# Two modulation chunks moved into dead tiles piece by piece, output weights awaited by halves, one value projection cut in two, and the first tile's store moved behind the last gather

## What is computed

```python
mod = silu(c) @ w_ada + b_ada
sh1, sc1, g1, sh2, sc2, g2 = split(mod, 6)
h = x * (1 + sc1) + sh1
qa, ka, va, qb, kb, vb = split(h @ w_in)
ya = rms_norm(moba_attention(qa, ka, va, bias))
yb = rms_norm(dilated_attention(qb, kb, vb, bias))
x = layer_norm(ALPHA * x + (1 + g1) * (concat(ya, yb) @ w_out))
h2 = x * (1 + sc2) + sh2
# router: 8 heads, top 16 of 128 x 128 product keys
q = h2 @ w_q
s1, s2 = q @ sub_keys, top 16 of each, top 16 of their 256 sums -> e, g
f = sum over 128 experts (gelu(h2 . u[e]) * g) * v[e]
x = layer_norm(ALPHA * x + (1 + g2) * f)
```

## Time and profile before

| | |
|---|---|
| device time, median of 3 runs | 826.3 us (824.68, 826.3, 827.65) |
| the profiled execution: time / span | 824.76 us / 823.0 us |
| busy share: TensorE, VectorE, ScalarE, GpSimd | 83%, 71%, 41%, 36% |
| gathers (GpSimd's queue) | 268.45 MB |
| all other loads and stores (SP's queue) | 54.55 MB |
| mean DMA rate over the span | 393 GB/s |

### The profile page before, as it was taken

How to read it: one execution, slowest core, us unless ns; L and a number is a source line. 1 busy time by engine, 2 the same in 40 slices (tenths; PEclk the granted TensorE clock), 3 DMA queues, 4 the chain that set the end, 5 groups by cost and what they waited for, 6 DMA issues and landing times.

```text
span 823.0 us, 7304 instructions
## 1 busy us (share of the span) xinstructions
PE 686.9 (83%) x1984; PEld 326.1 (40%) x1984; DVE 583.0 (71%) x1348; ACT 340.5 (41%) x989; POOL 295.0 (36%) x262
## 2 busy tenths in 40 slices
PE   8999979899997979696989777877868787878785
PEld 4887635554444544352323223322322222223221
DVE  4666967877798777777777878757675767675455
ACT  0012323476646343444445345444343434353333
POOL 1000000234346545454455443544344443434330
PEclk9999989999999989899989997999999999999999
DMA  9999995699999999999999999999999999999992
GB/s 304 376 403 413 420 418 207 261 347 374 385 392 411 422 421 422 421 422 421 422 421 422 420 422 412 406 423 421 422 422 420 422 422 421 420 422 422 422 420 93
DMA packets 56925, 323.74 MB, mean 393 GB/s; under 512 B 6130, under 2 KB 16690, under 8 KB 20402
## 3 DMA queue, kind: packets, MB, share of 16 engines
q0 software_dynamic: 37008, 268.45, 79.2%
q1 hardware_dynamic: 18994, 54.55, 17.2%
q10 hardware_dynamic: 882, 0.27, 0.2%
HBM read 322.18 MB, written 1.07 MB: 393 GB/s over the span
## 4 chain that ended last, share of the span: by engine, by line
DMA 48%; PE 34%; DVE 8%; issue 4%; ACT 4%; POOL 1%; DVEq 0%; SPq 0%; ACTq 0%
DMA ring<-in_experts,e_all 45%; PE bank L518 19%; PE bank L507 7%; PE bank L540 4%; DMA ring<-in_w 4%; DVE acc L1008 3%; DVE ring L858 3%; ACT diag L707 1%; PE bank L622 1%; PE bank L603 1%; POOL ring L1160 1%; ACT weight L698 1%; ACT gel L694 1%; PE bank L610 1%; DVE T_h L871 0%
## 5 line engine op out<-in xcount | busy, mean ns | idle before, releaser
L518 PE MATMUL bank<-ring,diag 128*128 128x512 f32 x952 | 475.5, 636 | 107.9 <-ACT diag L707 107.1
L1160 POOL DMA_INDIRECT ring<-in_experts,e_all x255 | 289.1, 1134 | 501.2 <-PE bank L518 297.1
L518 PEld LDWEIGHTS bank<-ring,diag 128*128 128x128 f32 x952 | 174.7, 198 | 387.3 <-ACT diag L707 228.2
L858 DVE CUSTOM_DVE_ANT_0 ring<-ring,T_h 128x1024 f32<-128x1024 f32 x128 | 156.7, 1225 | 111.7 <-DMA ring<-in_experts,e_all 111.7
L858 DVE CUSTOM_DVE_ANT_0 ring<-ring,h 128x1024 f32<-128x1024 f32 x128 | 156.7, 1224 | 70.8 <-DMA ring<-in_experts,e_all 68.6
L694 ACT ACTIVATE gel<-pre 128x1 f32<-128x1 f32 x256 | 51.8, 202 | 327.8 <-DVE pre L858 327.2
L707 ACT ACTIVATE diag<-consts,weight 128x128 f32<-128x128 f32 x238 | 95.5, 401 | 7.8
L698 ACT ACTIVATE weight<-gel,g_all 128x1 f32<-128x1 f32 x256 | 75.4, 295 | 9.3
L1008 DVE SCALAR_TENSOR_TENSOR acc<-ring,cact,acc 128x512 f32<-128x512 f32 x63 | 47.4, 752 | 5.8 <-DMA ring<-in_w 3.0
L507 PE MATMUL bank<-ring,hT_yT 128*128 128x512 f32 x80 | 35.6, 596 | 0.8 <-DMA ring<-in_w 0.7
L540 PE MATMUL bank<-hT_yT,lnw 128*128 128x256 f32 x128 | 28.7, 380 | 0.9 <-DVE hT_yT L975 0.9
(11 more groups left out here) (178 smaller groups left out, 556.3 us busy)
## 6 DMA issues: line engine op xcount, KB each, us to landing
ring<-in_w SPq DMA_DIRECT2D x18, 1024.0 KB, 13.7
ring<-in_w SPq DMA_DIRECT2D x12, 512.0 KB, 10.5
H_s<-in_w SPq DMA_DIRECT2D x6, 1024.0 KB, 14.4
ring<-in_w SPq DMA_DIRECT2D x16, 256.0 KB, 7.0
lnw<-in_w SPq DMA_DIRECT2D x4, 1024.0 KB, 17.3
ring<-in_experts,e_all POOLq DMA_INDIRECT x255
H_s<-in_w SPq DMA_DIRECT2D x5, 512.0 KB, 9.1
lnw<-in_w SPq DMA_DIRECT2D x4, 512.0 KB, 8.5
```

The source lines that it names most:

```text
L518: last = nc.tensor.matmul(tile_sum(t)[n], diag[:, m % DIAGS, :], ring[:, RING_AT[i], D + CH * n:D + CH * n + CH], start=(s == 0), stop=(s ...
L858: nc.vector.tensor_tensor_reduce(ring[:, r, 0:D], ring[:, r, 0:D], h2[i // SLOTS], 1.0, 0.0, ALU.mult, ALU.add, pre[:, i % PAIR:i % PAIR + ...
L1160: nc.gpsimd.indirect_dma_start(ring[:, r, :], None, A["experts"], bass.IndirectOffsetOnAxis(ap=e_all[:, i:i + 1], axis=0)).then_inc(slot_i ...
```

## The change

1. Chunk 10 is no longer loaded into the ring. It comes in three pieces: 2 rows into `QT_h2T[:, 0:D]`, 2 into `hT_yT[:, 0:D]`, 4 into `H_s[:, 0:2D]`. Chunk 11's pieces are 2 rows in xT_y, 1 in V_x1, 1 in diag, 4 in `H_s[:, 2D:4D]`.
2. Their sums are cut: `wsuma 11` (4 rows), `wsuma 10 0` and `wsuma 10 1` (2 each), later `wsumb 10` and `wsumb 11` (4 each). `patch_read` counts them, and loads and copies that reuse the tiles wait for its values.
3. SP's list is reordered; the output chunks are loaded, and awaited by `wo`, by halves.
4. `v 1 1` is split: 6 of its 8 k steps (`va`) stay ahead of `ln1b`, the last 2 follow the scores `s 0 0`.
5. In PLAN, `wo 0 0 1` comes after `yT 0 1`; `rows2` after `xa 0`; `S 4` goes behind `early`; `Tr 4` behind `madd 7`.
6. The stores of tile 0 wait for the last gather of values.

Cut to its core:

```diff
-          ("ada", 6), ("in", 4), ("ada", 7), ("ada", 8), ("in", 5), ("ada", 9), ("out", 0), ("ada", 10), ("out", 1), ("q", 0),
-          ("ada", 11), ("q", 1)]
+READ_HIGH, READ_LOW, READ_ALL = 3, 4, 5
+          ("ada", 6), ("in", 4), ("ada", 7), ("ada", 8), ("in", 5), ("ada", 9), ("out", 0), ("out", 1), ("q", 0),
+          ("ada", 10), ("ada", 11), ("q", 1)]
-AFTER_HEAD0 = [("S", 5), ("PV", 4), ("piece", 1, 0), ("v", 0, 1), ("gelu",)]
+AFTER_HEAD0 = [("Tr", 4), ("S", 5), ("PV", 4), ("piece", 1, 0), ("v", 0, 1), ("gelu",)]
-       ("modrow", 4), ("madd", 4), ("Tr", 2), ("Tr", 3), ("wo", 0, 0, 0), ("PV", 2), ("PV", 3), ("wsum", 10), ("ny", 0), ("modrow", 5), ("madd", 5),
-       ("wo", 0, 0, 1), ("yT", 0, 1), ("rows2",), ("xa", 0), ("wo", 0, 1, 0), ("wo", 0, 1, 1), ("ln1a", 0),
-       ("v", 1, 1), ("ln1b", 0), ("wsum", 11), ("hT", 0, 0), ("hT", 0, 1), ("S", 4), ("q", 0, 0), ("wsumb", 11),
-       ("s", 0, 0, 0), ("s", 0, 0, 1), ("modrow", 6), ("Tr", 4), ("madd", 6), ("modrow", 7)]
-    + [("piece", 0, j) for j in range(5)] + [("early",)] + [("piece", 0, j) for j in range(5, EXP_PIECE)]
+       ("modrow", 4), ("madd", 4), ("Tr", 2), ("Tr", 3), ("wsuma", 11), ("wo", 0, 0, 0), ("wsuma", 10, 0), ("PV", 2), ("PV", 3), ("ny", 0), ("modrow", 5), ("madd", 5),
+       ("yT", 0, 1), ("wo", 0, 0, 1), ("xa", 0), ("wsuma", 10, 1), ("wo", 0, 1, 0), ("rows2",), ("wo", 0, 1, 1), ("ln1a", 0),
+       ("va", 1, 1), ("ln1b", 0), ("hT", 0, 0), ("hT", 0, 1), ("wsumb", 10), ("wsumb", 11), ("q", 0, 0),
+       ("s", 0, 0, 0), ("s", 0, 0, 1), ("v", 1, 1), ("modrow", 6), ("madd", 6), ("modrow", 7)]
+    + [("piece", 0, j) for j in range(5)] + [("early",), ("S", 4)] + [("piece", 0, j) for j in range(5, EXP_PIECE)]
+VA_STEPS = 6
...
             load(("ada", 9))
-            load(("out", 0))
+            load(("out", 0), (0,))
+            sp.wait_ge(hT_ready, KC)
+            for i in range(3):
+                load_patch(11, i)
             filled(sp, ("qk", 3, 1))
-            load(("out", 1))
-            summed(sp, 8)
-            load(("ada", 10))
+            load(("out", 1), (0,))
+            load(("out", 0), (1,))
+            filled(sp, ("S", 3))
+            load_patch(10, 0)
+            sp.dma_start(x[:], A["x"].rearrange("(t p) c -> p t c", p=P)).then_inc(x_in, 16)
+            load(("out", 1), (1,))
+            filled(sp, ("v", 1, 0))
+            load_patch(10, 1)
             summed(sp, 9)
-            sp.wait_ge(hT_ready, KC)
             sp.dma_start(ln1.rearrange("p r c -> p (r c)"), A["ln"][:, 0:2 * D].broadcast_to([P, 2 * D])).then_inc(ln1_in, 16)
-            sp.dma_start(x[:], A["x"].rearrange("(t p) c -> p t c", p=P)).then_inc(x_in, 16)
...
-            summed(sp, 10)
+            load_patch(10, 2)
             load(("q", 0))
-            filled(sp, ("v", 1, 0))
+            sp.wait_ge(rows2_ready, 1)
+            load_patch(11, 3)
+            sp.wait_ge(patch_read, READ_HIGH)
             load_part("high", 0)
-            filled(sp, ("S", 3))
             load_part("high", 1)
-            sp.wait_ge(rows2_ready, 1)
+            sp.wait_ge(patch_read, READ_ALL)
             load_part("high", 2)
-            sp.wait_ge(patch_read, 1)
             load_part("low", 0)
...
+            sp.wait_ge(values_in, 16)
             for t in range(NT):
...
-                    w = chunk(pe, ("out", n))
+                    arrived(pe, CHUNK[("out", n)], g)
+                    w = places[W_PLACES[CHUNK[("out", n)]]]
...
-                    act.wait_ge(patch_read, 1)
+                    act.wait_ge(patch_read, READ_LOW)
```

More of the change, by code:

```diff
@@ L153 @@
 STEP_BANKS = 6
-NO_FILL = ("early", "qkz", "qkh", "warm", "wsumb", "gelu", "ny", "xa", "rows2", "ln1a", "ln1b", "x1", "piece", "madd", "wsum", "dot", "slot", "fold", "ln2a", "ln2b", "ln2c")
+NO_FILL = ("early", "qkz", "qkh", "warm", "wsumb", "gelu", "ny", "xa", "rows2", "ln1a", "ln1b", "x1", "piece", "madd", "wsum", "wsuma", "dot", "slot", "fold", "ln2a", "ln2b", "ln2c")
 OPENED = [("qk",) + s[1:] for s in PLAN if s[0] == "qkz"]
-FILLS = OPENED + [s for s in PLAN if s[0] not in NO_FILL and s not in OPENED]
+BEGUN = {("va",) + s[1:]: s for s in PLAN if s[0] == "v" and ("va",) + s[1:] in PLAN}
+FILLS = OPENED + [BEGUN.get(s, s) for s in PLAN if s[0] not in NO_FILL and s not in OPENED and s not in BEGUN.values()]
 APART = [("bias",)] + [("modc", h) for h in range(QUARTERS)] + [("wo", 0, 1, n) for n in range(2)]
@@ L229, in build @@
         ln1 = H_s[:, NT * D:].rearrange("p (r c) -> p r c", r=2)
-        patches = [H_s[:, 0:2 * D].rearrange("p (k n) -> p k n", n=CH), xT_y[:, D:2 * D].rearrange("p (k n) -> p k n", n=CH), V_x1[:, 1:2, 0:CH],
-                   diag[:].rearrange("p (r i) c -> p r (i c)", r=1)]
-        patch_of = [(i, k) for i, patch in enumerate(patches) for k in range(patch.shape[1])]
+        rows_of = lambda part: part.rearrange("p (k n) -> p k n", n=CH)
+        patches = {10: [rows_of(QT_h2T[:, 0:D]), rows_of(hT_yT[:, 0:D]), rows_of(H_s[:, 0:2 * D])],
+                   11: [rows_of(xT_y[:, D:2 * D]), V_x1[:, 1:2, 0:CH], diag[:].rearrange("p (r i) c -> p r (i c)", r=1), rows_of(H_s[:, 2 * D:4 * D])]}
+        patch_of = {c: [(i, k) for i, patch in enumerate(patches[c]) for k in range(patch.shape[1])] for c in patches}
         acc = sb("acc", [P, 4, CH])
@@ L296, in build @@
         patch_read = sem("patch_read")
-        patch_in = [sem(f"patch_in{i}") for i in range(len(patches))]
+        patch_in = {c: [sem(f"patch_in{c}_{i}") for i in range(len(patches[c]))] for c in patches}
         wq_in = {"high": sem("wq_high_in"), "low": sem("wq_low_in")}
@@ L449, in _, with load_patch @@
             load(("in", 5))
+            def load_patch(c, i):
+                src = A["w"][CHUNK[("ada", c)]].rearrange("p (k n) -> p k n", k=KC)
+                n = patch_of[c].index((i, 0))
+                sp.dma_start(patches[c][i], src[:, n:n + patches[c][i].shape[1]]).then_inc(patch_in[c][i], 16)
             summed(sp, 7)
             load(("ada", 9))
-            load(("out", 0))
+            load(("out", 0), (0,))
+            sp.wait_ge(hT_ready, KC)
+            for i in range(3):
+                load_patch(11, i)
             filled(sp, ("qk", 3, 1))
-            load(("out", 1))
-            summed(sp, 8)
-            load(("ada", 10))
+            load(("out", 1), (0,))
[6 more added lines that the diff above has]
+            load_patch(10, 1)
             summed(sp, 9)
-            sp.wait_ge(hT_ready, KC)
             sp.dma_start(ln1.rearrange("p r c -> p (r c)"), A["ln"][:, 0:2 * D].broadcast_to([P, 2 * D])).then_inc(ln1_in, 16)
-            sp.dma_start(x[:], A["x"].rearrange("(t p) c -> p t c", p=P)).then_inc(x_in, 16)
[L461 to L464, removed]
-            summed(sp, 10)
+            load_patch(10, 2)
             load(("q", 0))
@@ L569, in _ @@
                     continue
-                dst, full = open_bank(step) if step not in OPENED else (bank[PLACE[step][0]], bank_full[PLACE[step][0]])
+                if step in OPENED or step in BEGUN.values():
+                    dst, full = bank[PLACE[step][0]], bank_full[PLACE[step][0]]
+                else:
+                    dst, full = open_bank(BEGUN.get(step, step))
                 if kind == "bias":
@@ L581, in _ @@
                     projection(dst, c, i, [h for h in range(QUARTERS) if ("qkh", h, c, i) not in PLAN]).then_inc(full, 1)
-                elif kind == "v":
+                elif kind in ("v", "va"):
                     g, t = step[1:]
                     w = chunk(pe, ("in", 2 + 3 * g))
-                    product(dst[:], lambda k: hT[:, k, t, :], lambda k: w[:, k, :]).then_inc(full, 1)
+                    split = VA_STEPS if ("va", g, t) in PLAN else 0
+                    for k in range(split) if kind == "va" else range(split, KC):
+                        last = nc.tensor.matmul(dst[:], hT[:, k, t, :], w[:, k, :], start=(k == 0), stop=(k == KC - 1))
+                    if kind == "v":
+                        last.then_inc(full, 1)
                 elif kind == "lnb":
@@ L746, in _ @@
                     if t == 1 and g == 0:
-                        summed(act, 11)
+                        act.wait_ge(patch_read, 1)
                     evacuate(step, V_x1[:, t, CH * g:CH * g + CH], filled(act, step)[:])
@@ L976, in _ @@
                                                 ALU.mult, ALU.add).then_inc(hT_ready, 1)
-                elif kind in ("wsum", "wsumb"):
+                elif kind in ("wsum", "wsuma", "wsumb"):
                     c = step[1]
                     n = CHUNK[("ada", c)]
-                    patched = c == 11
+                    patched = c in patches
                     part = acc[:, c % 4, :]
-                    ks = range(KC // 2) if kind == "wsum" and ("wsumb", c) in PLAN else range(KC // 2, KC) if kind == "wsumb" else range(KC)
-                    if kind == "wsum":
```

(14 more changed lines are left out.)

2 lines of the change are left out of this document (1 added, 1 removed).

## The result

The changed kernel takes 831.1 us (four runs, 830.13 to 831.45) where the kernel before takes 826.45 in the same comparison: ratio 1.0056, 95% interval 1.0036 to 1.0076. It is 4.7 us **slower**. The forecast was 827.0, "no change", with a range up to 830. The profiled execution took 831.11 us, span 829.3, so 6.3 more than the span before. The profiled execution of the kernel before (824.76) lies 1.7 us under its median, so the pair of traces shows more than the medians do.

A forecast was written before the change was run, and what follows sets the result against it. DMA was taken to be full late (600 to 780 us), with TensorE holding the chain to 214.85 us. A later `v 0 1` (+2.0) and late stores (-1.25) gave +0.7 on 826.3: 827.0 us, range 822 to 830.

The forecast's parts named there:

- When the pieces land, and VectorE up to h2: Loads and VectorE's chain: chunk 10's first piece lands at 110.4, `PV` reads end at 113.3, h2 at 132.5 (before 133.3).
- rival D: Loads: each piece pays a fixed cost in series, first piece at 116.4, `v 0 1` 6 us later, 833 us; chance 0.03.
- rival B: First piece lands before 108, TensorE never stands, h2 at 129.4, `v 0 1` ends at 157.5, 823.9 us; chance 0.08.
- The first fall of the clock: TensorE stands 4.1 us until 113.5, then its clock falls in `wo 0 0 1`: 1.5 us, between 0 and 2.2.
- TensorE from h2 to `v 0 1`: 21.4 us as before plus 1.1, 1.8 and 2.3 for moved work and waits: 26.6, so `v 0 1` ends at 160.6.
- The clock behind h2: TensorE between h2 and `v 0 1`: no clock fall in the sum, a second fall left to rival C.
- rival C: A second clock fall between h2 and `v 0 1`: up to 2.2 us more, 829.9 with the full first fall; chance 0.13.
- After `v 0 1` the list is the same: Behind `v 0 1` TensorE holds the chain to 214.85, so its 2.0 us delay reaches the end in full.
- A gap of 3.24 us kept 1.00: TensorE's clock in the kernel before: full after 3.24 us idle, but 0.50 after 4.66 us; used to size the first fall.
- The first gather: Gather 0 at 146.8, 2.6 us earlier; the fifth at 161; the saving is DMA idle time moved, not removed.
- The stores: Two stores (0.5 MB) leave the full stream at 518 us for the tail: minus 1.25 us, or 0 if hidden.
- Rival A: The end follows the first gather and the filled hole counts: -2.6 - 1.25, 822.4 us; chance 0.22.

The follow-up runs named there:

- e11: The changed kernel run once more, nothing altered: 831.85 us, ratio 1.005 to the kernel before.
- e3: The changed kernel with `v 1 1` in one piece ahead of `ln1b`: 830.53 us, ratio 1.0051 to the kernel before.
- e7: The changed kernel with `v 1 1` whole and `S 4`, `Tr 4` back at their old places: 822.43 us, ratio 0.9949 to the kernel before.
- the pair with the clock held: e9_all_heat against e10_wlate_heat, which differ only in the order behind h2: 818.3 and 824.15 us.
- e6: The changed kernel with `v 1 1` whole, `S 4` and `Tr 4` back, chunk 10's first pair of sums behind `yT`: 822.83 us, ratio 0.996 to before.
- e12: The changed kernel with 4 idle-time matmuls ahead of `yT` alone: 827.38 us, ratio 1.0012 to the kernel before.
- e1: The kernel before with one edit, the stores of tile 0 wait for the last gather: 825.08 us, ratio 0.998.
- e2: The changed kernel with chunk 10's first pair of sums moved behind `yT`: 825.58 us, ratio 0.9982 to the kernel before.
- e5_heat: The changed kernel with idle-time matmuls, 4 ahead of `yT`, 1 of `hT`, 3 of `PV 5`: 824.24 us, ratio 0.9971 to the kernel before.
- e10_wlate_heat: The changed kernel with chunk 10's first pair behind `yT` and idle-time matmuls ahead of `hT` (4) and `PV 5` (3): 824.15 us, ratio 0.9977 to before.
- e13_wait_heat: e9_all_heat with chunk 10's first pair ahead of `PV` again, idle-time matmuls ahead of `yT` (4) and `PV 5` (3): 819.03 us, ratio 0.99 to before.
- e9_all_heat: e6 plus idle-time matmuls, 3 ahead of `hT` and 3 ahead of `PV 5`: 818.3 us, ratio 0.9918 to the kernel before.

## Why the prediction was wrong

- **When the pieces land, and VectorE up to h2:** right (110.6, 113.5, 132.9). Small pieces cost nothing of their own, so rival D is out, and rival B too, since the first piece landed after 108. The 2.0 us behind rival D stand in the Trainium skill ("DMA: Bandwidth & Descriptors", Anatomy of one DMA) as a fit to DMAs that GpSimd issued; the pieces here were issued by SyncE.
- **The first fall of the clock:** right in place; the size (1.6 for 1.5) was luck. The same eight matmuls behind much the same gap (4.49 to 4.53 us) took 6.06, 6.15 and 5.88 us in e11, e3 and e7, so 2.3 to 2.6 over 3.60, above the 2.2 that was taken as a full fall.
- **TensorE from h2 to `v 0 1`:** the added 5.2 us are shown as 5.0 by the pair with the clock held. The waits themselves can be read: `modrow 6` starts at 143.82, 0.68 us after it could, and `S 5` waits 0.86 for `madd 7`; `s 0 1` waits 0.61 where it was 0.55, so the 0.5 forecast there was not paid.
- **The clock behind h2: here it failed.** The sum put the falls there at nothing, and left them to rival C at 0.13. The profiled execution has 1.6 in `q 0 0`; with 0.4 at h2 that is all that lies between 160.6 and 162.6.
- **"After `v 0 1` the list is the same ... I carry the 2.0 us on in full":** the second failed step. The list was the same but not its clock. "A gap of 3.24 us kept 1.00" rested on one execution; the same 3.24 us were followed by a slow `PV 5` or slot 0 in both profiles of the changed kernel and in e3, e6, e7 and e12, and not in before, e1 and e2. In the profile here it put gather 6 another 2.6 us later (0.86 in `PV 5`, 1.8 in slot 0). Rival C is what happened, twice over, at a chance that was far too low.
- **How far these two terms fill the miss:** on the scale of the profile the forecast was 825.5 and 831.11 was measured, 5.6 more. 0.4, 1.6 and 2.6 make 4.6; 1.5 more are lost between gathers 6 and 149, and 0.5 more than forecast comes back behind. That 1.6 and 2.6 also make the 4.1 between the medians 827.0 and 831.1 is no proof, since in e7_v_s4 the same fall at `PV 5` was made up by gather 30. In the changed kernel it was not (gather 30 is 7.0 us later than before); one more fall lies there at 212.79 us, a slot of 5.29 us for 3.81.
- **The first gather:** forecast 146.8, measured 149.2, outside the 146 to 148 named as a sign. 2.0 of the 2.4 us are again h2 and the fall in `q 0 0`.
- **The stores:** 1.1 measured by the medians, 1.25 forecast.
- **Rival A** (the end follows the first gather) is out: in e2_wsuma_late it came 3.5 us earlier than in before, `v 0 1` 0.7 later, and the time is that of e1_store.

So the 4.7 us are: +5.0 from the order behind h2; less 2.0 because `hT` starts at 133.04 instead of 135.08 (what the split and the pieces bought, 0.6 of it a first fall of 1.6 instead of 2.2), less 0.6 between `hT` and `q 0 0`, less 1.1 for the stores: 1.3 us, close to the forecast 0.7. The rest, 3.4, I put down to the clock; that is an attribution and not a measurement. The idle-time matmuls gain 6.9 us in the changed kernel and 4.9 in the kernel before, which supports 2 of it as the clock's share in the difference, and leaves 1.4 that are not located. By the ratios the two gains are 7.0 and 3.6 us, which would cover all of it; the runs do not decide between the two.

**Open.** Between e5_heat and e10_wlate_heat the wait for the piece is removed and the medians are equal (824.24, 824.15), as between e7_v_s4 and e6_all. In the second pair the trace shows the fall that ate most of it; in the first `v 0 1` ended 4.1 us earlier and only the profiled runs differ (826.99 and 822.52). In the traces of e13_wait_heat and e9_all_heat half of a delay there is absorbed before gather 149; what absorbs it I did not find, nor why the delay grows in the changed kernel.

## What to carry to other kernels

A step that only moves work earlier should be checked at the engine that ends the stage, here TensorE, and not at the transfer that it lets start: `S 4`, the tail of `v 1 1` and three small bank and copy waits on the short path behind h2 cost more than an earlier h2 and free queue gave. Keep what fills another engine's latency (`S 4` under the copies of `hT`) where it is when something else is moved; undo such a group as a whole, since undoing one of it showed nothing. When TensorE has idle stretches of a few microseconds ahead of dense work, price the fall of its clock behind every one of them, and try cheap matmuls into a free bank: here they were worth 0.4 to 0.9% in each of three kernels (the lower figure by the ratios), and e9_all_heat at 818.3 us is the fastest of the study.

## What the runs showed of the hardware that was not expected

- Whether the clock falls behind a given gap differs between executions of the same program: `q 0 0` 5.44 us in one profile of the changed kernel and 3.81 in another, `v 0 1` 7.09 and 9.16.
- A gap of 3.24 us was followed by matmuls slowed wholly or in part (`PV 5` or slot 0) in six of nine profiles; one of 2.62 us (e6_all, ahead of `hT`) too, by 6.13 us for a `q 0 0` of 3.84.
- Seven matmuls of no use, 6 us of TensorE's time in idle stretches, made the kernel before, with its stores late, faster by 4.9 us (3.6 by the ratios).
